# A two-layer hybrid decoder step on one core: low halves of the dense weights written in place, four high halves, more PSUM banks, a rearranged first norm, full-row value products, and a second layer without its meta tokens

## The chip, the cores and the metric

The kernel runs on one core of one Trainium2 chip. The metric is the device time of one execution in microseconds (us). Before the change three runs gave a median of 1439.03 us (1437.47 to 1439.14).

## The reference, cut to what matters

336 token columns go through two layers with the same weights: 16 learned meta tokens, 256 prompt tokens (together one sequence of 272), and 8 samples of 8 new tokens each. Only the prompt tokens and the samples are returned as `y`; of the meta tokens the outputs hold nothing directly.

```python
def mixer_block(x, pos, attend, conv_prev, h_prev, p, l):
    hn = rmsnorm(x, p['ln_mix'][l])
    z = hn @ p['w_in'][l]                       # q, k, v, recurrent x, recurrent gate y, two merge gates
    att, k_state, v_state = attend(l, q, k, v, p['attn_sinks'][l])   # window of 128, sink softmax
    rec, h_last, conv_state = rglru_branch(xr, conv_prev, h_prev, pos, ...)   # conv of 4, two gates, scan
    rec = rec * jax.nn.gelu(yr)
    merged = jax.nn.sigmoid(ga) * (att @ p['w_att_proj'][l]) + jax.nn.sigmoid(gr) * (rec @ p['w_rec_proj'][l])
    return x + merged @ p['w_out'][l], k_state, v_state, conv_state, h_last

for l in range(DEPTH):                          # DEPTH = 2
    x, ... = mixer_block(x, ..., l)
    hf = rmsnorm(x, p['ln_ffn'][l])
    x = x + swiglu(hf, ...) if l % 2 == 0 else x + moe_ffn(hf, ...)   # layer 1: top 2 of 8 experts
return rmsnorm(x, p['ln_final']), ...
...
y_prompt = y_p[:, N_META:]
```

In layer 1 the keys, the values and the recurrent x of the meta tokens are still needed by the prompt tokens behind them (window and scan); their merge gates, their y, their attention output and their merged x are not.

## The kernel before, in words

All activations lie with the features on the 128 partitions and the tokens as columns. Every dense product is made in three passes of rounded 32-bit matmuls (fp32r): a weight w is split into a high part (w rounded to fp32r) and a low part (w less that), an activation likewise, and `three` issues high x high, high x low and low x high into one PSUM bank. The weights stream from HBM in chunks of 512 KB (128 x 1024 values: 8 tiles of 128 x 128). For each chunk c:

- SyncE loads it into one of four `raw` buffers (`RING = 4`). It may load over a slot when the low part of the chunk four before is done (`lo_done`).
- ScalarE's `hi(c)` rounds it into one of two `whi` buffers (`SPLIT = 2`), which must have been released by TensorE: it waits until chunk c-2 is multiplied (`pe_chunk`).
- VectorE's `lo(c)` subtracts and writes one of two `wlo` buffers. In the gate stage `hi_lo(c)` does both on VectorE.
- TensorE's `chunk(c)` makes 24 matmuls, 3 for each tile, and raises `pe_chunk`.

A layer's chunks are numbered: 20 for k, v, recurrent x and q (0 to 19), 16 merge gates, 8 for the block-diagonal gates of the recurrence (`N_G`, 360 columns each), 10 for y (`C_Y`), 8 attention projection (`C_A`), 10 recurrent projection (`C_R`), 8 output projection (`C_O`). After layer 0 come 72 chunks of the dense FFN; after layer 1 the router and the experts, with their own rings (`mraw`, `mwhi`; there the low part `mwlo` is already written over `mraw`).

Each engine's program is written out in a fixed order; engines meet through semaphores alone. What matters for the change:

- First norm. The first 12 chunks multiply x times the gain, unnormalised, and VectorE scales the result by 1/rms afterwards. Layer 0's sum of squares is made on ScalarE (`square`), added on GpSimd (`add_squares`), summed over partitions on TensorE inside chunk 2 (`sums`), and goes through `root` (ScalarE) and `reciprocal` (VectorE). Four banks hold the results until then. VectorE then also computes `softplus` of a small tensor in one piece in step 9.
- Attention, step s: TensorE makes scores of unit s+1, one weight chunk, `turn(s)` (transposes of the weights) and `values(s-1)`. VectorE makes `maxima`, `weights`, `lo` and in some steps `conv(t)`, one tenth of the convolution. 17 units of kinds A, B, C, D. In C and D the values of the new tokens (`vp[0:16, 2]`, `vnew` with 8 rows) are multiplied with 16 or 8 rows of the array, between products with 128 rows.
- Recurrence. While the y and attention-projection chunks run, ScalarE makes three functions per tenth (`factors`), a square root in two pieces and the gelu of `yr` in two halves; VectorE multiplies and scans; GpSimd multiplies hs by yr (`rect`); ScalarE and VectorE split `rect` into `rech` and `recl`, which the recurrent projection reads. VectorE also takes each chunk's result out of PSUM, and does that ahead of `lo(c+2)`. Two banks alternate.

Of the kernel before, what the change touches and what calls it, by code (L numbers as in the profile page):

```python
# [18 lines left out]
F32 = mybir.dt.float32  # L19
# [7 lines left out]
P = 128  # L27
# [43 lines left out]
RING, SPLIT = 4, 2  # L71
# [16 lines left out]
ATT_N = {"A": 4, "B": 2, "C": 2, "D": 2}  # L88
SINK0 = {"A": 0, "B": 16, "C": 32, "D": 34}
# [25 lines left out]
def build_step(nc, w_mix, w_ffn, w_moe, x_in, consts_in, par_in, misc_in, state_in, kc_in, vc_in,  # L115
               o_y, o_kp, o_vp, o_ks, o_vs, o_state):
    with ExitStack() as ctx:
# [29 lines left out]
        vnew = at("vnew", [SS, SB, P], F32, I_)  # L147
# [110 lines left out]
        k_ready, vt_mm, v_ready = sem("k_ready"), sem("vt_mm"), sem("v_ready")  # L258
# [50 lines left out]

        def gain(n):  # L310
            return lnf if n == 4 else p_(n // 2, "ln_ffn" if n % 2 else "ln_mix")

        def att_part(u):
# [7 lines left out]
            first = 2 * P if kind == "C" else TP + 16 * i  # L321
            return qkx[:, 0:KD, first:first + 16], o[:, 0:P].rearrange("p (h s) -> p h s", h=KD)
# [5 lines left out]
        def _(sy):  # L328
            sy.dma_start(raw[:, 0, :], w_mix[0, 0]).then_inc(raw_loaded[0], 16)
# [3 lines left out]
            sy.dma_start(raw[:, 1, :], w_mix[0, 1]).then_inc(raw_loaded[1], 16)  # L333
            sy.dma_start(cst[:, 0:256], consts_in[:, 0:256]).then_inc(consts_loaded, 16)

            def stream(src, c0, n):

                first = 0
                if c0 == 0:
                    for j in range(2, RING):  # L340
                        sy.dma_start(raw[:, j, :], src[j]).then_inc(raw_loaded[j], 16)
# [3 lines left out]
                with sy.Fori(first // 4, n // 4) as i:  # L345
                    for j in range(4):
                        sy.wait_ge(lo_done, i * 4 + (c0 + j + 1 - RING))
                        sy.dma_start(raw[:, (c0 + j) % RING, :], src[i * 4 + j]).then_inc(raw_loaded[(c0 + j) % RING], 16)
# [3 lines left out]
            stream(w_mix[1], BASE[1], N_MIX)  # L352
# [3 lines left out]
            for j in range(MRING):  # L356
                if j == N_EARLY:
# [22 lines left out]
        def _(pool):  # L380
# [11 lines left out]
            for l in range(2):  # L392
# [21 lines left out]

                pool.wait_ge(z_evac, z0 + 1)
# [20 lines left out]
                pool.dma_start(o_vs[l, WIN - SS:WIN], vnew[:, :, :]).then_inc(kv_out_done, 16)  # L436

                pool.wait_ge(o_evac, NU * (l + 1))
                for k in range(KD):
                    pool.wait_ge(att_hi, 2 * l + k // 4 + 1)  # L440
                    pool.tensor_tensor(attl[:, k, :], qkx[:, k, :], atth[:, k, :].bitcast(F32), ALU.subtract).then_inc(att_lo, 1)

                for t in range(KR):
# [3 lines left out]
                    pool.tensor_tensor(rect[:, t, 0:TP], hs[:, t, 0:TP], yr[:, t, 0:TP], ALU.mult)  # L447
# [1502 lines left out]
```

## Time and profile before

| | |
|---|---|
| median of 3 runs | 1439.03 us |
| the profiled execution: its own time | 1435.18 us |
| its span (first to last instruction) | 1433.3 us |
| granted TensorE clock, mean | 0.996 |
| TensorE busy / VectorE / ScalarE / GpSimd | 97% / 75% / 58% / 11% |

A page of the profile groups instructions by line and tile. Two things are needed to read it here. The ends of matmuls are modelled and overlap their successors: a 336-column matmul is shown with 0.32 us, but the next one starts 0.153 us later, so the rate is read from starts, not from durations. And an idle time in front of a matmul is counted from that modelled end, so the matmul starts later than an unbroken stream would have it by the idle time and about 0.16 us more.

### The profile page before, as it was taken

Reading aid. Unit: us, or ns where it says so; the run is one execution under the profiler, and the core shown is the slowest. Engines: PE = TensorE matmul, PEld = TensorE weight load, DVE = VectorE, ACT = ScalarE, POOL = GpSimd, SP = SyncE. Lnnn points to the kernel's source line nnn. Section 1 sums busy time; section 2 is a strip of 40 time slices with the busy share of each in tenths; the row PEclk is TensorE's granted clock in tenths of the full one; section 3 lists DMA queues with packets and bytes.
Section 4 is the critical chain, followed back from the end, with each engine's and each line's share of the span. In section 5 each row is a group of like instructions: output and inputs, shape, how many; then the busy total and the mean of one; then the engine's idle time right before and its main releaser. Section 6 shows DMA issues by size and latency. Waiting matters only on the chain.

```text
span 1433.3 us, 24028 instructions
## 1 busy us (share of the span) xinstructions
PE 1388.4 (97%) x8258; PEld 1267.7 (88%) x8258; DVE 1081.6 (75%) x1593; ACT 827.9 (58%) x1221; POOL 155.1 (11%) x175
## 2 busy tenths in 40 slices
PE   6999999899999999999999999999999999999997
PEld 5988899899999999999888998996888888888885
DVE  5678776977666664556687769765998998998987
ACT  4356547734433333343565477345888888888884
POOL 2010002311100000100000023112120120011010
PEclk9999999999999999999999999999999999999999
DMA  6443244354545454444332344468999999999991
GB/s 231 132 136 103 89 118 147 118 151 136 178 138 144 145 146 138 141 146 140 131 104 89 118 147 118 145 234 296 401 396 385 408 367 368 409 374 369 401 334 54
DMA packets 83256, 298.28 MB, mean 208 GB/s; under 512 B 9568, under 2 KB 10848, under 8 KB 83168
## 3 DMA queue, kind: packets, MB, share of 16 engines
q1 hardware_dynamic: 77760, 278.39, 56.1%
q0 software_dynamic: 5408, 18.72, 4.3%
q8 instruction: 55, 0.90, 0.3%
q14 instruction: 33, 0.27, 0.1%
HBM read 285.50 MB, written 11.58 MB: 207 GB/s over the span
## 4 chain that ended last, share of the span: by engine, by line
PE 79%; DVE 13%; issue 4%; ACT 3%; POOL 0%; DMA 0%; ACTq 0%; DVEq 0%; SPq 0%; POOLq 0%
PE ps L1385 17%; PE ps L1387 17%; PE ps L1386 17%; PE ps L1676 7%; PE ps L1680 7%; PE ps L1677 7%; DVE mwlo L940 3%; DVE wlo L875 3%; ACT whi L531 1%; PE ps L1484 1%; DVE hs L1088 1%; ACT mwhi L531 1%; PE ps L1500 1%; PE ps L1460 1%; DVE htl L1345 1%
## 5 line engine op out<-in xcount | busy, mean ns | idle before, releaser
L875 DVE TENSOR_TENSOR wlo<-raw,whi 128x1024 fp32r<-128x1024 f32 x232 | 288.5, 1243 | 185.1 <-ACT whi L531 184.3
L531 ACT ACTIVATE whi<-raw 128x1024 fp32r<-128x1024 f32 x216 | 228.5, 1058 | 335.9 <-PE ps L1387 332.9
L940 DVE TENSOR_TENSOR mwlo<-mraw,mwhi 128x1024 fp32r<-128x1024 f32 x290 | 345.0, 1222 | 35.2 <-ACT mwhi L531 30.4
L531 ACT ACTIVATE mwhi<-mraw 128x1024 fp32r<-128x1024 f32 x290 | 304.1, 1060 | 61.5 <-PE ps L1680 59.1
L1385 PE MATMUL ps<-xuh,whi 128*128 128x336 f32 x576 | 184.6, 320 | 12.5 <-DVE xul L887 8.0
L1386 PE MATMUL ps<-xul,whi 128*128 128x336 f32 x576 | 182.7, 317 | 0.0
L1387 PE MATMUL ps<-xuh,wlo 128*128 128x336 f32 x576 | 182.5, 317 | 0.0
L1385 PE MATMUL ps<-xnh,whi 128*128 128x336 f32 x544 | 176.7, 325 | 4.8 <-DVE wlo L875 4.0
L1387 PE MATMUL ps<-xnh,wlo 128*128 128x336 f32 x544 | 172.4, 317 | 0.0
L1386 PE MATMUL ps<-xnl,whi 128*128 128x336 f32 x544 | 172.0, 316 | 0.0
L1676 PE MATMUL ps<-mwhi,xeh 128*128 128x512 f32 x384 | 152.7, 398 | 0.9 <-ACT xeh L531 0.9
L1680 PE MATMUL ps<-mwhi,xel 128*128 128x512 f32 x384 | 149.9, 390 | 0.0
L1677 PE MATMUL ps<-mwlo,xeh 128*128 128x512 f32 x384 | 149.6, 390 | 0.0
L1385 PEld LDWEIGHTS ps<-xuh,whi 128*128 128x128 f32 x576 | 109.4, 190 | 13.3 <-issue 8.0
L1385 PEld LDWEIGHTS ps<-xnh,whi 128*128 128x128 f32 x544 | 102.3, 188 | 14.5 <-issue 12.0
L1386 PEld LDWEIGHTS ps<-xul,whi 128*128 128x128 f32 x576 | 109.7, 190 | 0.3
L1387 PEld LDWEIGHTS ps<-xuh,wlo 128*128 128x128 f32 x576 | 109.4, 190 | 0.0
L1386 PEld LDWEIGHTS ps<-xnl,whi 128*128 128x128 f32 x544 | 102.6, 189 | 0.0
L1387 PEld LDWEIGHTS ps<-xnh,wlo 128*128 128x128 f32 x544 | 102.1, 188 | 0.0
L1680 PEld LDWEIGHTS ps<-mwhi,xel 128*128 128x128 f32 x384 | 72.1, 188 | 15.8 <-DVE xel L1308 0.4
L1676 PEld LDWEIGHTS ps<-mwhi,xeh 128*128 128x128 f32 x384 | 72.2, 188 | 15.0 <-issue 1.1
L1677 PEld LDWEIGHTS ps<-mwlo,xeh 128*128 128x128 f32 x384 | 72.2, 188 | 14.0
(310 smaller groups left out, 2667.7 us busy)
## 6 DMA issues: line engine op xcount, KB each, us to landing
mraw<-w_moe SPq DMA_DIRECT2D x292, 512.0 KB, 8.0
raw<-w_mix SPq DMA_DIRECT2D x160, 512.0 KB, 3.6
raw<-w_ffn SPq DMA_DIRECT2D x72, 512.0 KB, 3.6
x<-x_in SPq DMA_DIRECT2D x4, 336.0 KB, 5.6
tok_d<-xt POOLq DMA_DIRECT2D x6, 224.0 KB, 4.8
ysum_d<-zero POOLq DMA_DIRECT2D x3, 448.0 KB, 10.9
ysum<-ysum_d POOLq DMA_DIRECT2D x3, 448.0 KB, 10.2
o_y<-nt SPq DMA_DIRECT2D x8, 168.0 KB, 1.9
```

Source lines behind the costliest of these rows:

```text
L531: return nc.scalar.activation(out, in_, ACT.Copy)
L875: v.tensor_tensor(wlo[c % SPLIT][:, :, :], raw[:, c % RING, :].rearrange("p (k n) -> p k n", n=P), f32(whi[c % SPLIT][:, :, :]), ALU.subtr ...
L940: v.tensor_tensor(mwlo[q % MRING][:, :, :], mraw[q % MRING][:, :].rearrange("p (k n) -> p k n", n=512), f32(mwhi[q % MSPLIT][:, :, :]), AL ...
L1088: v.tensor_tensor_scan(hs[:, t, :], rg[:, t, :], ig[:, t, :], 0.0, ALU.mult, ALU.add).then_inc(scan_done, 1)
L1345: v.tensor_tensor(htl[n % 2][:, :, :], ps[4][:, :].rearrange("p (k n) -> p k n", k=4), f32(hth[n % 2][:, :, :]), ALU.subtract).then_inc(ht ...
L1385: mm(out, wh, xh, start=start, stop=False)
L1386: mm(out, wh, xl, start=False, stop=False)
L1387: return mm(out, wl, xh, start=False, stop=stop)
L1460: ins = mm(bank[:, 0:256], qkx[r, k, 128:256], qkx[r, 8, 0:256], start=True, stop=True)
L1676: mm(out, lhs_h, hi[:, n, :], start=start, stop=False)
L1677: mm(out, lhs_h, lo[:, n, :], start=False, stop=False)
L1680: return mm(out, lhs_l, hi[:, n, :], start=False, stop=stop)
```

## The change

- `lo` writes `wlo` over its own `raw` slot; the freed room makes four `whi`. `hi` waits for TensorE no more (its slot is free when the new chunk has been loaded); the load itself now waits for `pe_chunk` of the chunk four before instead of `lo_done`. The last four chunks of layer 1 are loaded between the first expert loads.
- The first 12 chunks use 6 banks instead of 4; layer 0's sum of squares goes from chunk 2 to chunk 3; chunks 4 and 5 are split ahead of the root; `softplus` is spread over three steps. y and attention projection use 4 banks, the recurrent projection two others.
- In y, the projections and the output VectorE does `lo(c+2)` ahead of taking chunk c's result. `conv(1)` leaves step 16 of the projections; `conv(1)` to `conv(8)` stand at steps 3, 6, 9, 11, 13, 15, 17, 18 of the attention.
- `vp[:, 2]` and `vnew` get 128 rows, cleared by GpSimd, and the value products of units C and D use all of them. A D unit's output is laid out by sample, so that it is contiguous.
- In layer 1, from the merge gates on, the 16 meta columns are left out (`kept(l)`): 320 columns instead of 336.

```diff
-RING, SPLIT = 4, 2
+RING = 4
+N_BANKS = 6
+CONV_AT = (3, 6, 9, 11, 13, 15, 17, 18)
...
-        raw = at("raw", [P, RING, CH], F32, 10752)
-        whi = [at(f"whi{i}", [P, 8, P], F32R, 27136 + 8192 * i) for i in range(SPLIT)]
-        wlo = [at(f"wlo{i}", [P, 8, P], F32R, 31232 + 8192 * i) for i in range(SPLIT)]
+        raw = [at(f"raw{i}", [P, CH], F32, 10752 + 4096 * i) for i in range(RING)]
+        wlo = [at(f"wlo{i}", [P, 8, P], F32R, 10752 + 4096 * i) for i in range(RING)]
+        whi = [at(f"whi{i}", [P, 8, P], F32R, 27136 + 4096 * i) for i in range(RING)]
...
+        def kept(l):
+            return slice(META if l else 0, T)
... SyncE
-                        sy.wait_ge(lo_done, i * 4 + (c0 + j + 1 - RING))
+                        sy.wait_ge(pe_chunk, i * 4 + (c0 + j + 1 - RING))
...
+                if j in (4, 6, 8, 10):
+                    c = N_MIX - RING + j // 2 - 2
+                    sy.wait_ge(pe_chunk, BASE[1] + c + 1 - RING)
+                    sy.dma_start(raw[(BASE[1] + c) % RING][:, :], w_mix[1, c])...
... GpSimd
+                pool.wait_ge(pe_chunk, BASE[l] + N_U)
+                if l == 0:
+                    pool.memset(vp[:, 2, :], 0.0).then_inc(v_zero, 1)
+                pool.memset(vnew[:, :, :], 0.0).then_inc(v_zero, 1)
... ScalarE, hi
-                if c >= SPLIT:
-                    act.wait_ge(pe_chunk, i * step + (c - SPLIT + 1))
-                copy(whi[c % SPLIT][:, :, :], raw[:, c % RING, :]...
+                copy(whi[c % RING][:, :, :], raw[c % RING][:, :]...
... ScalarE, start of layer 0
             hi(3)
+            act.wait_ge(eps_set, 1)
+            nc.scalar.activation(rms3[:, 0:1], eps[:, :], ACT.Sqrt)
+            hi(4)
+            hi(5)
... VectorE, first norm
-                    if l == 0 and j == 0:
-                        lo(c0 + 3)
+                    else:
+                        for c in {0: (2, 3, 4, 5), 1: (6,), 3: (7,)}.get(j, (j + 3,) if 5 <= j <= 10 else ()):
+                            lo(c)
... VectorE, y (attention projection alike)
+                    lo(c0 + C_Y + t + 2)
                     ve.wait_ge(pe_chunk, c0 + C_Y + t + 1)
-                    v.tensor_copy(yr[:, t, :], ps[t % 2][:, 0:T]).then_inc(z_evac, 1)
-                    lo(c0 + C_Y + t + 2)
+                    v.tensor_copy(yr[:, t, kept(l)], ps[t % 4][:, kept(l)]).then_inc(z_evac, 1)
... TensorE, values
                         elif kind == "C":
-                            few = TP - 256
                             mm(ps[7][r, 0:128], vp[:, 1, r], pt[q][:, g, :], start=True, stop=False)
-                            ins = mm(ps[7][r, 0:128], vp[0:few, 2, r], pt[q][0:few, 2 + g, :], start=False, stop=True)
+                            ins = mm(ps[7][r, 0:128], vp[:, 2, r], pt[q][:, 2 + g, :], start=False, stop=True)
                         else:
                             for i in range(2):
-                                out = ps[7][r, 0:128].rearrange("p (h i s) -> p h i s", i=2, s=SS)[:, :, i, :]
+                                out = ps[7][r, 64 * i:64 * i + 64]
                                 mm(out, vc[:, b, r], pt[q][:, i, r], start=True, stop=False)
-                                ins = mm(out, vnew[:, b, r], pt[q][0:SS, 2 + i, r], start=False, stop=True)
+                                ins = mm(out, vnew[:, b, r], pt[q][:, 2 + i, r], start=False, stop=True)
... TensorE, merge gates of layer 1 (y and the projections alike)
-                        chunk(c0 + C_I + s, ps[s % 2][:, 0:T], xnh, xnl)
+                        tokens = kept(l) if s >= 2 else slice(0, T)
+                        chunk(c0 + C_I + s, ps[s % 2][:, tokens], xnh[:, :, tokens], xnl[:, :, tokens])
```

Where the order of an engine's instructions moves, at the two places on which most rests. First VectorE at the start of layer 0, in the kernel before (`wlo` is the low part of a chunk, `rstd` the reciprocal, `qkx<-ps,rstd` the scaled result of a chunk, `nt` and `xnl` the norm of one feature tile):

```order
L875 TENSOR_TENSOR wlo_53<-raw,whi_51 128x1024
L875 TENSOR_TENSOR wlo_54<-raw,whi_52 128x1024
L892 RECIPROCAL rstd<-rms 128x336
L967 TENSOR_TENSOR qkx<-ps,rstd 128x336
L895 SCALAR_TENSOR_TENSOR nt<-x,par,rstd 128x336
L967 TENSOR_TENSOR qkx<-ps,rstd 128x336
L895 SCALAR_TENSOR_TENSOR nt<-x,par,rstd 128x336
L900 TENSOR_TENSOR xnl<-nt,xnh 128x336
L875 TENSOR_TENSOR wlo_53<-raw,whi_51 128x1024
```

And the same place now:

```order
L898 TENSOR_TENSOR wlo_56<-raw_52,whi_60 128x1024
L898 TENSOR_TENSOR wlo_57<-raw_53,whi_61 128x1024
L898 TENSOR_TENSOR wlo_54<-raw_50,whi_58 128x1024
L898 TENSOR_TENSOR wlo_55<-raw_51,whi_59 128x1024
L914 RECIPROCAL rstd<-rms 128x336
L995 TENSOR_TENSOR qkx<-ps,rstd 128x336
L917 SCALAR_TENSOR_TENSOR nt<-x,par,rstd 128x336
L898 TENSOR_TENSOR wlo_56<-raw_52,whi_60 128x1024
```

The low parts of chunks 4 and 5 moved from behind the reciprocal and the first evacuations to ahead of it.

Second, VectorE in the attention projection of a layer (`gates<-ps,gates` takes a chunk's result out, `hs` is the scan, `recl` the low part of the recurrent output), before:

```order
L1116 TENSOR_TENSOR gates<-ps,gates 128x336
L875 TENSOR_TENSOR wlo_54<-raw,whi_52 128x1024
L1108 TENSOR_TENSOR recl<-rect,rech 128x336 x3
L1088 SCALAR_TENSOR_TENSOR hs<-rg,ig 128x360 x2
L1116 TENSOR_TENSOR gates<-ps,gates 128x336
L875 TENSOR_TENSOR wlo_53<-raw,whi_51 128x1024
L1108 TENSOR_TENSOR recl<-rect,rech 128x336 x2
```

And now:

```order
L898 TENSOR_TENSOR wlo_57<-raw_53,whi_61 128x1024
L1143 TENSOR_TENSOR gates<-ps,gates 128x336
L1134 TENSOR_TENSOR recl<-rect,rech 128x336 x3
L1114 SCALAR_TENSOR_TENSOR hs<-rg,ig 128x360 x2
L898 TENSOR_TENSOR wlo_54<-raw_50,whi_58 128x1024
L1143 TENSOR_TENSOR gates<-ps,gates 128x336
L1134 TENSOR_TENSOR recl<-rect,rech 128x336 x2
```

The low part of chunk c+2 stands ahead of the wait for chunk c, where it stood behind.

## Rows read from the trace of the kernel before

**Rows 1.** The page: each engine's busy us, share of the span, instructions.
```profile
PE 1388.4 (97%) x8258; PEld 1267.7 (88%) x8258; DVE 1081.6 (75%) x1593; ACT 827.9 (58%) x1221; POOL 155.1 (11%) x175
```

**Rows 2.** Windows: length, busy us (count) of PE, PEld, DVE, ACT, POOL, PEclk, DMA, GB/s.
```profile
400.00:600.00 200.00, 200.00 (x1307) 200.00 (x1306) 117.46 (x164) 71.75 (x85) 4.43 (x4) 1.00 0.48 144
256.00:295.00 39.00, 34.71 (x217) 32.95 (x217) 38.06 (x46) 26.24 (x36) 19.43 (x23) 1.00 0.43 128
866.00:905.00 39.00, 34.72 (x217) 32.95 (x216) 38.01 (x46) 26.23 (x36) 19.42 (x23) 1.00 0.44 129
```

**Rows 3.** Timeline of TensorE, first norm: start, us, line, tiles, shape [idle before <-releaser].
```profile
23.01 0.83 PE L1392 MATMUL ps<-acc,cst 128*128 128x336 f32 x2 [2.38 <-POOL acc L390]
...
31.83 0.42 PE L1385 MATMUL ps<-xuh,whi 128*128 128x336 f32 x1 [3.86 <-DVE wlo L875]
...
32.90 0.48 PE L1387 MATMUL ps<-xuh,wlo 128*128 128x336 f32 x1
33.18 0.48 PE L1385 MATMUL ps<-xuh,whi 128*128 128x336 f32 x1
...
63.83 0.41 PE L1385 MATMUL ps<-xnh,whi 128*128 128x336 f32 x1 [0.83 <-DVE qkx L967]
```

**Rows 4.** Windows at the attention's start, both layers; then VectorE's timeline there.
```profile
80.00:106.00 26.00, 24.36 (x175) 22.43 (x175) 19.83 (x51) 14.45 (x48) 0.51 (x1) 1.00 0.34 103
134.00:155.00 21.00, 21.00 (x153) 18.63 (x150) 18.37 (x50) 12.47 (x36) 0.00 (x0) 1.00 0.33 101
690.00:716.00 26.00, 22.98 (x163) 21.17 (x163) 18.44 (x49) 14.31 (x45) 0.52 (x1) 1.00 0.27 89
...
89.03 0.46 DVE L987 TENSOR_SCALAR xc<-ext,par 128x360 f32<-128x360 f32 x1
...
92.25 1.22 DVE L875 TENSOR_TENSOR wlo<-raw,whi 128x1024 fp32r<-128x1024 f32 x1
```

**Rows 5.** Timeline of TensorE: value products of units B, C, D, and what follows.
```profile
155.72 0.67 PE L1500 MATMUL ps<-pt,vp 128*64 128x128 f32 x8
156.32 0.33 PE L1458 MATMUL ps<-kc,qt 64*64 64x136 f32 x2
...
166.83 0.43 PE L1503 MATMUL ps<-pt,vp 128*64 128x128 f32 x2
...
168.27 0.33 PE L1458 MATMUL ps<-kc,qt 64*64 64x136 f32 x2
...
173.23 0.33 PE L1509 MATMUL ps<-pt,vc 128*64 128x64 f32 x2
...
175.28 0.45 PE L1458 MATMUL ps<-kc,qt 64*64 64x136 f32 x4
```

**Rows 6.** Timeline of TensorE: idle in gate stage, y stage, and start of the FFN.
```profile
208.54 0.43 PE L1385 MATMUL ps<-xch,whi 128*128 128x360 f32 x1 [0.76 <-DVE wlo L875]
...
229.36 0.39 PE L1385 MATMUL ps<-xnh,whi 128*128 128x336 f32 x1 [0.30 <-DVE wlo L875]
...
373.83 0.42 PE L1385 MATMUL ps<-xuh,whi 128*128 128x336 f32 x1 [0.58 <-DVE wlo L875]
```

**Rows 7.** Timelines of ScalarE and GpSimd: the recurrence's chain in layer 0.
```profile
271.71 1.61 ACT L714 ACTIVATE yr<-yr 128x1680 f32<-128x1680 f32 x1
...
273.40 0.79 POOL L447 TENSOR_TENSOR rect<-hs,yr 128x272 f32<-128x272 f32 x1 [29.41 <-ACT yr L714]
...
291.20 0.60 POOL L448 TENSOR_TENSOR rect<-hs,yr 128x64 f32<-128x64 f32 x1
```

**Rows 8.** Timeline of TensorE in the gate stage, first and last of 20 matmuls.
```profile
202.82 0.32 PE L1386 MATMUL ps<-xcl,whi 128*128 128x360 f32 x1
...
205.96 0.33 PE L1387 MATMUL ps<-xch,wlo 128*128 128x360 f32 x1
```

**Rows 9.** The page: weight loads, count, KB each, median us from issue to landing.
```profile
mraw<-w_moe SPq DMA_DIRECT2D x292, 512.0 KB, 8.0
raw<-w_mix SPq DMA_DIRECT2D x160, 512.0 KB, 3.6
```

More of the change, by code:

```diff
@@ L900, in normal_low, with softplus @@
                 v.tensor_tensor(xnl[:, k, :], nt[:, k, :], f32(xnh[:, k, :]), ALU.subtract).then_inc(xlo_done, 1)
-            def softplus():
+            def softplus(part):
                 a, b = PAR["lam"]
@@ L907, in softplus @@
                 two = lambda t: t[:, :].rearrange("p (l k) -> p l k", l=2)
-                v.scalar_tensor_tensor(out=two(sp_e), in0=lam, scalar=-1.0, in1=lam, op0=ALU.mult, op1=ALU.max).then_inc(c_ready, 1)
-                step(v.tensor_scalar(two(sp_q), lam, -1.0, 0.0, ALU.mult, ALU.max))
-                a, b = PAR["sinks"]
-                step(v.tensor_scalar(nsink[:, :].rearrange("p (l k) -> p l k", l=2), par[:, :, a:b], -1.0, None, ALU.mult))
-                ve.wait_ge(sp_exp, 1)
-                step(v.tensor_scalar(sp_p[:, :], sp_e[:, :], 2.0, None, ALU.add))
@@ L914, in softplus @@
-                step(v.reciprocal(sp_z[:, :], sp_p[:, :]))
-                step(v.tensor_tensor(sp_z[:, :], sp_z[:, :], sp_e[:, :], ALU.mult))
-                step(v.tensor_tensor(sp_e[:, :], sp_z[:, :], sp_z[:, :], ALU.mult))
-                step(v.tensor_scalar(sp_p[:, :], sp_e[:, :], 1.0 / 15, None, ALU.mult))
-                for d in (13, 11, 9, 7, 5, 3):
-                    step(v.scalar_tensor_tensor(out=sp_p[:, :], in0=sp_p[:, :], scalar=1.0 / d, in1=sp_e[:, :], op0=ALU.add, op1=ALU.mult))
@@ L971, in _ @@
                         normal_low(l, j - 1)
-                    if l == 0 and j == KD + 1:
-                        softplus()
+                    if l == 0 and j > KD:
+                        softplus(j - KD - 1)
                 def lines():
@@ L1051, in _ @@
                         lo(c0 + C_I + s + 1)
-                    if s % 3 == 0 and 3 <= s <= 15:
-                        conv(1 + s // 3)
-                    if s >= 17:
-                        conv(s - 10)
+                    if s in CONV_AT:
+                        conv(CONV_AT.index(s) + 1)
                     if s == 5:
@@ L1131, in _ @@
                     c = c0 + C_R + j
+                    lo(c + 2)
                     done = m < KD and (KR * m + KR - 1) // 8 == j
@@ L1401, in chunk @@
                         sum_squares(sums)
-                    ins = three(out, whi[c % SPLIT][:, k, :], wlo[c % SPLIT][:, k, :], xh[:, k, :], xl[:, k, :],
+                    ins = three(out, whi[c % RING][:, k, :], wlo[c % RING][:, k, :], xh[:, k, :], xl[:, k, :],
                                 start and k == 0, stop and k == 7)
@@ L1407, in _ @@
                 c0, u0 = BASE[l], NU * l
[L1408 to L1417 removed]
+                for j in range(N_U):
+                    if j >= N_BANKS:
+                        pe.wait_ge(z_evac, N_IN * l + j - N_BANKS + 1)
+                    if l == 0 and j == 3:
+                        pe.wait_ge(consts_loaded, 16)
+                    chunk(c0 + j, ps[j % N_BANKS][:, 0:T], xuh, xul, ready=None if j else xu_lo, count=16 * l,
+                          sums=2 * l if j == (0 if l else 3) else None)
                 pe.wait_ge(xlo_done, KD * (l + 1))
[L1419 to L1422 removed]
+                for j in range(N_U, C_I - 2):
+                    pe.wait_ge(z_evac, N_IN * l + j - 1)
+                    chunk(c0 + j, ps[j % 2][:, 0:T], xnh, xnl)
                 pe.wait_ge(z_evac, N_IN * l + 2)
```

185 lines of the change are left out of this document (95 added, 90 removed).

## The prediction, made before the changed kernel had run

> **What bounds the kernel now.** I read the page first: TensorE is busy 97% of the span [rows 1], no other engine comes near. In the windows, a stretch without a wait (the FFN) shows 1307 matmuls in 200 us, 0.153 us each, at the full clock [rows 2]. So two things shorten this kernel: less work on TensorE, or fewer of its waits. Then I listed TensorE's idle time in the timeline. It sits at few places: the first norm [rows 3], the start of the attention [rows 4], single waits at the gate and y stages and at the FFN [rows 6], and above all the stretch 256 to 295 and its twin in layer 1, where 217 matmuls, 33.5 us of work at 154.5 ns (that stage's rate), take 39 us [rows 2]. Last, the attention's value products: TensorE is called busy there, but the starts show that it advances slowly [rows 5].
>
> The sum is made against the profiled execution (1435.2 us with 1.9 us around its span); the median is 3.8 us above it, and I add the same to the forecast. Each wait is charged as its idle time plus 0.16 us for the modelled tail of the matmul before.
>
> **The change, part by part.**
>
> First norm. Chunk 2 waits 2.38 us for GpSimd's sums, chunk 4 waits 3.86 us for the low part that stands behind the reciprocal, and after that gap TensorE's granted clock is at the lower level: starts 0.28 us apart instead of 0.153, for some twelve matmuls [rows 3]. Now the sum stands at the end of chunk 3 (about 24 us; the sums were ready at 23.0, and ScalarE reaches its squares earlier), and six banks carry TensorE over chunks 4 and 5 to 32.7 us. By then VectorE must have lo(4), lo(5), the reciprocal, one result and lo(6). Chunk 4's load is issued when chunk 0 is multiplied (13.6 us), and lands beside the cache loads, say by 21; hi(5) by 24, root by 26, reciprocal by 28.5, lo(6) by 31. That fits with 1.7 us to spare. Gain: 2.54 + 4.02 + 12 x 0.13 = 8.1 us. The wait at 63.83 (0.83) is for chunk results held up by `softplus` in one piece; with it in three: 1.0 us. Together 9.1; at least 6.0, if the root is 3 us later than I think.
>
> Start of the attention. The idle time is 1.64 us in layer 0 (two waits) and 3.02 in layer 1 (three) [rows 4]. VectorE does conv(1) from 89.03 to 92.25, 3.2 us, just ahead of the low part and the maxima that TensorE wants [rows 4]. Gone from there, no wait is left: 4.66 + 5 x 0.16 = 5.5 us. The convolutions now stand denser from step 9 on. A stretch of 21 us, 3.8 steps with one convolution, has VectorE busy 18.4 us [rows 4]; with one in every second step it is 18.4 + 0.9 x 3.2 = 21.3 us of work in 21 us. That just fits, since the units C and D behind it cost VectorE less. At least 3.
>
> Value products. B units: four products of 128 columns, all with 128 rows, and the next line starts 0.60 us after the first (the two heads' chains side by side, 8 records). C: the same columns, but 128 and 16 rows by turns, 1.44 us. 
>
> The trace shows that loads with equal rows run ahead and those with changing rows don't. The Trainium skill ("TensorE: Matmul & The Clock Gate", Part 3, the mechanism) says nearly the opposite: a weight load overlaps a running matmul only when its row group differs. By that rule full rows win nothing, and the sum is 12.9 us less; the B and C rows speak against it.
>
> Gate and y stages. A wait of 0.76 in each layer, where `hi_lo` waits for TensorE and conv(9) follows, and 0.30 and about 0.2 in y [rows 6]; with four high parts ready ahead they go: 2 x (0.92 + 0.84) = 3.5 us; at least 1.5. The FFN's start waits 0.58 for a low part behind the reciprocal [rows 6]: 0.7 us.
>
> Recurrence and projections. 5.5 us lost per layer, 11.0 in all [rows 2]. VectorE is busy 38.06 of the 39 us, so it matters whether its work can come earlier. Before the stretch it isn't full (in y it waits for hi, which waits for TensorE), and the order "result, then lo(c+2)" leaves the low part only 1.2 us between its hi and TensorE's need. The long chain is: square root and gelu on ScalarE (the gelu's first half from 271.7), GpSimd's ten products (273.4 to 291.8, full), recl [rows 7]. Without ScalarE's waits for TensorE I get the gelu done at 269 instead of 273.3, GpSimd's last product at 288, the last recl at 290; TensorE, unhindered, begins the recurrent projection at 288.1 and needs the last recl 4.1 us later. On the way the low parts of attention chunks 4 to 6 come 1 to 2.5 us ahead of need. In layer 1 TensorE is faster still, so some wait is left. I take 5.0 + 4.0 = 9.0 us. At least 0, at most 11.8 with the short wait for the banks at the projections' border, 0.4 us a layer.
>
> Layer 1 without meta columns. 16 merge gates, 10 y, 8, 10 and 8 projection chunks: 52 chunks of 24 matmuls, 1248. From 360 columns (0.165 us, [rows 8]) to 336 (0.153 to 0.1545, [rows 2]) a column costs 0.43 to 0.5 ns; at the full clock of 2.4 GHz it is 0.417. With 0.417 x 16 = 6.7 ns: 8.3 us; with 0.5, 9.9. I take 8.4. The other engines do 5% less there.
>
> In place low parts: nothing. The same subtraction is already written over its input in the expert stage, hidden behind matmuls as this one is. The last four loads of layer 1 stand behind four expert loads: at 8.0 us from issue to landing [rows 9] and issued one to four chunks after the output stage begins, each is there more than 5 us before its need. Nothing; the experts' own loads are issued a little later but with a ring of 24 to live on.
>
> Sum: 9.1 + 5.5 + 12.9 + 3.5 + 0.7 + 9.0 + 8.4 = 49.1 us. 1435.2 - 49 = 1386 profiled, 1390 for the median.
>
> **The rivals.**
>
> Rival 1: VectorE bounds the recurrence. For it speaks 38.06 of 39 us; against it the idle it has before. Then the 11 us of waits stay, and the 18 shorter chunks of y and attention projection in layer 1 bring nothing (18 x 0.16 = 2.9): 1390 + 9 + 3 = 1402.
>
> Rival 2: value products don't speed up, because the row change isn't the cause but the 64-column form or the accumulation: D's share gone, C's small: 1390 + 11 to 13 = 1402. For it: D differs from B in more than rows. Against: C differs from B in the rows alone. Rivals 1 and 2 together: 1414.
>
> Rival 3, slower: the ring of raw slots. A slot is now held until TensorE is through with the chunk, and the load is issued only then. Load, hi and lo (landing + 1.06 + 1.23) and the multiplication (3.67) must fit into four chunk times, 14.7 us: from a landing of 8.7 us on every chunk is late. At a landing of 12 us a chunk takes (12 + 2.3 + 3.7) / 4 = 4.5 us instead of 3.67, and 228 chunks lose about 187 us: 1577. It outweighs the 49 us from a landing of 9.6 us on. For it: expert loads land in 8.0 us under a crowd. Against: the dense loads land in 3.6 [rows 9] at half the DMA share.
>
> Rival 4: the change holds, but the new order brings waits of its own at the first norm (root late) and with the denser convolutions: 3 + 2.5 lost, 1396.
>
> **How the numbers follow.** The forecast 50%, with its own range 1385 to 1396 (value products 9.5 to 12.9, recurrence 6 to 11.8, columns 8.3 to 9.9). Rival 4 15%, rival 1 18%, rival 2 12%, rival 3 2%, rivals 1 and 2 together 3%. The range 1384 to 1404 leaves out rival 3, rivals 1 and 2 together, and parts of the others' tails. A difference under 0.2% (2.9 us) can't be told from none here. Faster takes everything but rival 3 and a small rest: 96%; same 2%; slower 2%.
>
> **What would show it.** In the profile after: no idle over 0.3 us on TensorE between 8 and 55 us, and the granted clock full from 12 us on; layer 0's recurrence some 17 us earlier than before. The value lines of C and D as groups of records 0.6 us long. Matmuls of 128x320 in layer 1, 0.146 to 0.148 us apart. The window that answers to 256:295 with 217 matmuls in about 34 us, VectorE nearly as full. The expert stage as long as before. I am wrong if TensorE's idle time in the recurrence stays near 4 us a layer (rival 1), if D's products still show starts 0.26 us apart (rival 2), or if waits for raw loads appear anywhere in the dense part (rival 3).

## The result, and the profile after

The changed kernel takes 1392.39 us (median of 4 runs, 1391.69 to 1394.02) where the kernel before took 1439.09 (4 runs on the same chip). The ratio is 0.968, 95% interval 0.9663 to 0.9696. The forecast was 1390, range 1384 to 1404.

The profiled execution took 1391.69 us (span 1389.9), against 1435.18 before: 43.5 us less, where the sum of the terms said 49.1. The medians differ by 46.7 us. That the two differ goes with the granted clock, below.

The page after, first the busy time of the engines, as in [rows 1], and the weight loads of [rows 9]:

```profile
PE 1361.3 (98%) x8258; PEld 1250.4 (90%) x8258; DVE 1074.4 (77%) x1593; ACT 824.5 (59%) x1222; POOL 158.0 (11%) x178
...
mraw<-w_moe SPq DMA_DIRECT2D x292, 512.0 KB, 8.1
raw<-w_mix SPq DMA_DIRECT2D x160, 512.0 KB, 3.6
```

TensorE runs as many matmuls in 27 us less of busy time; the rest of the gain is idle time. The dense loads land as fast as before, so that the ring of raw slots is no bound (rival 3).

Windows of the changed kernel (length, busy us and count of PE, PEld, DVE, ACT, POOL, then granted clock, DMA share, GB/s): the FFN, the first norm, and the stretches that answer to 256:295 and 866:905 of [rows 2]:

```profile
400.00:600.00 200.00, 200.00 (x1306) 200.00 (x1305) 112.62 (x153) 70.00 (x85) 5.52 (x6) 1.00 0.47 142
8.00:55.00 47.00, 47.00 (x292) 46.81 (x293) 34.11 (x56) 25.76 (x40) 12.96 (x13) 1.00 0.61 201
237.00:271.00 34.00, 31.29 (x200) 30.28 (x199) 33.02 (x40) 23.96 (x32) 17.08 (x18) 1.00 0.42 125
835.00:866.00 31.00, 27.63 (x182) 26.37 (x181) 30.09 (x39) 19.73 (x25) 20.30 (x23) 1.00 0.40 120
```

The FFN is as before (1306 matmuls in 200 us, 1307 before). The first norm has no idle time left, and no fall of the clock: the starts are 0.28 us apart until 12.6 us, where they were in the kernel before until 12.0, and 0.153 from there on. But the recurrence stretch still has 2.71 us without a matmul in layer 0 and 3.37 in layer 1, with VectorE busy 97% of it. There the forecast fell short. TensorE's waits after, by what ended them (line, releaser, us in total, times, longest):

```profile
PE ps L1407 <- DVE xul L909: 8.0, 1, 8.0
PE ps L1407 <- DVE wlo L898: 5.8, 5, 2.4
```

The 8.0 us are the start of the kernel. The five waits for low parts are all in the two recurrences. TensorE's timeline (start, us, line, tiles, shape, idle before) names them:

```profile
256.50 0.40 PE L1407 MATMUL ps<-atth,whi 128*128 128x336 f32 x1 [0.32 <-DVE wlo L898]
266.72 0.40 PE L1407 MATMUL ps<-atth,whi 128*128 128x336 f32 x1 [2.39 <-DVE wlo L898]
...
843.39 0.41 PE L1407 MATMUL ps<-atth,whi 128*128 128x320 f32 x1 [0.30 <-DVE wlo L898]
847.62 0.38 PE L1407 MATMUL ps<-atth,whi 128*128 128x320 f32 x1 [0.44 <-DVE wlo L898]
857.62 0.39 PE L1407 MATMUL ps<-atth,whi 128*128 128x320 f32 x1 [2.40 <-DVE wlo L898]
```

To place the gain I set the start of each chunk's last matmul side by side in both traces. The difference grows, stage by stage, as the third column says. The fourth and fifth tell what each part costs when it alone is undone (the experiments below), by the medians and by the chunks' ends; in the fifth the falls of the granted clock in the recurrences, 1.5 us each, are left out.

| stage | forecast | by the traces | undone alone, medians | undone alone, traces |
|---|---|---|---|---|
| first norm | 9.1 | 9.2 | 9.1 | 7.4 |
| attention start | 5.5 | 5.2 | 5.6 | 3.2 |
| value products C, D | 12.9 | 1.7 + 9.2 = 10.9 | 11.5 | 10.9 |
| gate and y stages, FFN start, borders of stages | 4.2 | 4.5 | with the next row: 8.8 | with the next row: 9.4 |
| recurrence and attention projection | 9.0 | 4.4 | | |
| 16 columns in layer 1 | 8.4 | 9.1 | 8.9 | 8.0 |
| sum | 49.1 | 43.3 | 43.9 | 38.9 |

### The profile page after: what moved, and what is told of

Its sections match the earlier page's. It is cut to its first block, busy times and chain, and to the rows that moved or that the text cites. A ratio compares the mean times of both kernels' runs of the same rounds, so it can differ in the third digit from the quotient of the medians.

```text
span 1389.9 us, 23721 instructions
## 1 busy us (share of the span) xinstructions
PE 1361.3 (98%) x8258; PEld 1250.4 (90%) x8258; DVE 1074.4 (77%) x1593; ACT 824.5 (59%) x1222; POOL 158.0 (11%) x178
## 4 chain that ended last, share of the span: by engine, by line
PE 85%; DVE 9%; issue 3%; ACT 2%; DMA 0%; ACTq 0%; DVEq 0%; SPq 0%
PE ps L1407 19%; PE ps L1409 19%; PE ps L1408 19%; PE ps L1694 8%; PE ps L1698 7%; PE ps L1695 7%; DVE mwlo L967 3%; DVE wlo L898 1%; PE ps L1502 1%; DVE hs L1114 1%; ACT mwhi L549 1%; PE ps L1478 1%; PE ps L1518 1%; DVE htl L1367 1%; DVE ig L1101 1%
## 5 line engine op out<-in xcount | busy, mean ns | idle before, releaser
L1407 PE MATMUL ps<-xnh,whi 128*128 128x336 f32 (+1 forms) x544 | 174.5, 321 | 0.0
L1409 PE MATMUL ps<-xnh,wlo 128*128 128x336 f32 (+1 forms) x544 | 170.7, 314 | 0.0
L1408 PE MATMUL ps<-xnl,whi 128*128 128x336 f32 (+1 forms) x544 | 170.6, 314 | 0.0
```

The lines of the kernel that those rows point to most:

```text
L1407: mm(out, wh, xh, start=start, stop=False)
L1408: mm(out, wh, xl, start=False, stop=False)
L1409: return mm(out, wl, xh, start=False, stop=stop)
```

## The experiments

Each kernel is the changed one with one edit. Differences are against its median of 1392.4. The kernel before, run beside each set, had medians of 1436.4 to 1436.9 (9 runs each) where it had 1439.1 beside the changed kernel, so a difference between sets is good to 2 or 3 us; a kernel with an edit worth nothing, the second one here, came out at 1392.1.

**Few rows again.**

```diff
-    ins = mm(ps[7][r, 0:128], vp[:, 2, r], pt[q][:, 2 + g, :], start=False, stop=True)
+    ins = mm(ps[7][r, 0:128], vp[0:few, 2, r], pt[q][0:few, 2 + g, :], start=False, stop=True)
...
-        ins = mm(out, vnew[:, b, r], pt[q][:, 2 + i, r], start=False, stop=True)
+        ins = mm(out, vnew[0:SS, b, r], pt[q][0:SS, 2 + i, r], start=False, stop=True)
```

> The changed kernel with the value products of units C and D on 16 and 8 rows again (the layout of D's output stays contiguous). Theory (the alternation of row counts makes each product start late): C units 0.86 us longer twice, D units 1.15 us longer eight times, as the two traces show: 10.9 us slower than the changed kernel, 1403, with D's starts 0.26 us apart. Rival (the form of D's output, or its accumulation, is the cause): D's share stays gained, only C's 1.7 us come back, 1394. Second rival (nothing of it counts, another wait takes it up): 1392.

Measured: 1403.84 us (1403.57 to 1407.47), 11.5 slower; ratio to the kernel before 0.9774 (0.976 to 0.9787). TensorE's timeline of one D unit in this kernel, to the scores behind it:

```profile
162.86 0.33 PE L1527 MATMUL ps<-pt,vc 128*64 128x64 f32 x2
163.12 0.32 PE L1528 MATMUL ps<-pt,vnew 8*64 8x64 f32 x2
163.37 0.33 PE L1527 MATMUL ps<-pt,vc 128*64 128x64 f32 x2
...
164.65 0.32 PE L1528 MATMUL ps<-pt,vnew 8*64 8x64 f32 x2
164.91 0.68 PE L1476 MATMUL ps<-kc,qt 64*64 64x136 f32 x8
```

Each product with another row count starts 0.26 us after the one ahead; the unit takes 2.05 us, as before. The same unit in the changed kernel:

```profile
161.34 0.33 PE L1526 MATMUL ps<-pt,vc 128*64 128x64 f32 x2
161.51 0.28 PE L1527 MATMUL ps<-pt,vnew 128*64 128x64 f32 x2
161.63 0.33 PE L1526 MATMUL ps<-pt,vc 128*64 128x64 f32 x4
...
162.24 0.68 PE L1476 MATMUL ps<-kc,qt 64*64 64x136 f32 x8
```

0.90 us. Rival 2 of the prediction is out.

**Strided output.** Full rows, but D's output laid out by head again.

```diff
-    out = ps[7][r, 64 * i:64 * i + 64]
+    out = ps[7][r, 0:128].rearrange("p (h i s) -> p h i s", i=2, s=SS)[:, :, i, :]
```

> The changed kernel with D's output laid out by head again, so that each product writes eight pieces of eight columns 16 apart, but all rows full. Theory (rows decide alone): no change, within 1 us of the changed kernel, 1392. Rival (the strided output decides): 8 x 1.15 = 9.2 us slower, 1401.6.

Measured: 1392.12 us (1391.43 to 1392.79); ratio 0.9687 (0.9674 to 0.97). The D unit takes 0.90 us with the strided output too. The contiguous layout brings nothing; the rows do it.

**All columns in layer 1.** `kept(l)` returns `slice(0, T)`.

> The changed kernel with all 336 columns in layer 1. Theory (time is columns, for TensorE sets the pace everywhere): 52 chunks x 0.15 to 0.20 us by the traces, 9.3 us slower, 1401.7, and every stage by its own share. Rival (part of it is lost in the waits of the recurrence, where VectorE is full, so that shorter chunks there bring nothing): the 18 chunks of y and attention projection of layer 1 contribute 2.9 us less, 1399, and the waits of layer 1's recurrence are shorter than with 320 columns by as much.

Measured: 1401.33 us (1400.78 to 1402.16), 8.9 slower; ratio 0.9753 (0.9739 to 0.9766). The stages show both theories at work. The 16 merge gates of layer 1 cost 0.19 us each and the y chunks 0.20, but over the eight chunks of attention projection the distance to the changed kernel grows by only 0.1 us, once 1.5 us for a fall of the clock is taken off. There shorter chunks only wait longer: about 1.2 us of the 9.3 expected are lost, the y chunks' share is not.

**The first norm undone**: four banks, the sum of squares in chunk 2, low parts of chunks 4 and 5 behind the reciprocal, softplus in one piece.

```diff
-N_BANKS = 6
+N_BANKS = 4
...
-            hi(4)
-            hi(5)
...
-                          sums=2 * l if j == (0 if l else 3) else None)
+                          sums=2 * l if j == (0 if l else 2) else None)
```

> The changed kernel with the first norm as it was: four banks, the sum of squares in chunk 2, the low parts of chunks 4 and 5 behind the reciprocal, softplus in one piece. Theory: the three waits and the drop of the granted clock come back, 9.2 us slower, 1401.6, with the granted clock near half between 31 and 36 us. Rival (the four high parts alone, which free ScalarE and VectorE from waiting for TensorE, remove most of it): 3 us slower or less, 1395.

Measured: 1401.45 us (1399.57 to 1401.9), 9.1 slower; ratio 0.9754 (0.9741 to 0.9768). Its windows at the first norm, PE alone (busy, count, granted clock, DMA share, GB/s):

```profile
30.00:32.00 2.00, 2.00 (x11) 0.80 0.00 0
32.00:34.00 2.00, 2.00 (x9) 0.50 0.00 0
34.00:36.00 2.00, 2.00 (x13) 0.85 0.00 0
```

The lower level is back. By the chunks' ends 7.4 us return by chunk 4 and nothing behind it. The wait for GpSimd's sums is 1.33 us where it was 2.38, and the wait at 63.83 in [rows 3] does not come back, though `softplus` stands in one piece again: another part of the change removes that one too, most likely the four high parts, which no run here shows alone. The profiled execution loses another 1.5 us to a fall of the clock in layer 0's recurrence, which the changed kernel's didn't have. So that the medians give 9.1, as the forecast said, is partly luck.

**The convolutions where they stood.**

```diff
-                    if s in CONV_AT:
-                        conv(CONV_AT.index(s) + 1)
+                    if s % 3 == 0 and 3 <= s <= 15:
+                        conv(1 + s // 3)
+                    if s >= 17:
+                        conv(s - 10)
```

> The changed kernel with the convolutions where they stood: conv(1) in the projections, the others from step 3 on by threes and in the last steps. Theory: the waits at the attention's start come back (1.9 us in layer 0, 3.1 in layer 1), 5 us slower, 1397.4, and TensorE idle near the start of the attention again. Rival (the four high parts give VectorE's low parts enough room anyway): 1 us, 1393.5.

Measured: 1398.02 us (1396.16 to 1398.44), 5.6 slower; ratio 0.9725 (0.9712 to 0.9738). By the chunks' ends 0.9 us come back in layer 0 and 2.3 in layer 1 at the attention's start, 3.2 of the 5 expected: a part of this gain stays without moving the convolutions. The profiled execution has a fall of the clock in each recurrence besides, 1.5 us apiece, which is more than the rest of the 5.6.

**The order undone in y and attention projection.**

```diff
-                    lo(c + 2)
                     ve.wait_ge(pe_chunk, c + 1)
...
                     v.tensor_tensor(gates[:, j, kept(l)], ps[j % 4][:, kept(l)], gates[:, j, kept(l)], ALU.mult)...
+                    lo(c + 2)
```

> The changed kernel with the order 'result, then low part of chunk c+2' again on VectorE in y and attention projection. Theory (the low part has only 1.2 us of slack behind the result, and VectorE is full from 251 to 277): the first waits of the recurrence grow by a low part's 1.2 us in several chunks, and the change loses 2 to 4 us, 1395.5. Rival (VectorE has the same work in either order, so the order moves waits but makes none): within 1 us, 1392.

Measured: 1397.44 us; ratio 0.9724 (0.971 to 0.9737). The five runs are 1392.98 (the profiled one, mean clock 0.998) and 1396.5 to 1397.7 (0.994 and 0.995). In the profiled one the chunks' ends slip 1.2 us in each layer's recurrence, 2.3 in all, which is within the theory; that the others are 4 us longer goes with their lower mean clock, but they have no trace.

**Two high parts again, the rest as changed.**

```diff
+                if c >= 2:
+                    act.wait_ge(pe_chunk, i * step + (c - 1))
                 copy(whi[c % RING][:, :, :], raw[c % RING]...
```

> The changed kernel with the high part waiting again until TensorE is through with chunk c-2, as it must with two buffers; all else as changed. Theory (this wait is what tied ScalarE and VectorE to TensorE and made the waits of gate stage, y and recurrence): the waits of the gate stage (0.9 a layer) and y (0.5 a layer) come back, and ScalarE's chain to the gelu is 3 to 5 us later, so that the recurrence waits 4 us more in all; 7 us slower, 1399, the first norm's gain partly lost beside it. Rival (the order and the banks made the gain, not the high parts): within 1.5 us, 1393.

Measured: 1420.44 us (1418.87 to 1421.11), 28 slower, not 7; ratio 0.9883 (0.9868 to 0.9898). Neither theory. TensorE's waits in this kernel, the four that say why:

```profile
PE ps L1410 <- DVE wlo L900: 9.7, 11, 2.4
...
PE ps L1410 <- DVE gates L1165: 4.8, 6, 1.1
...
PE ps L1410 <- issue: 3.0, 1, 3.0
PE ps L1410 <- DVE mgl L1170: 2.1, 2, 1.1
```

TensorE now waits for results and their splits (`gates`, `mgl`), which it doesn't in the changed kernel. The timeline without TensorE's own rows, inside the recurrent projection:

```profile
287.33 1.06 ACT L549 ACTIVATE whi<-raw 128x1024 fp32r<-128x1024 f32 x1 [2.23 <-PE ps L1412]
...
288.50 1.23 DVE L900 TENSOR_TENSOR wlo<-raw,whi 128x1024 fp32r<-128x1024 f32 x1 [1.68 <-ACT whi L549]
```

The high part waits for TensorE, the low part for the high part, and the result behind them can't begin before 289.7, 2.4 us after the high part was let go. Another 5.9 of the 28 us lie at the first norm: a wait of 3.0 us at 57.88 (the row `issue`), and behind it matmuls at the lower clock (granted 0.50 from 58 to 62 us). Then I put the order back too:

**Two high parts and the old order** (two high parts from chunk 14 on, so that the first norm stays as changed; the old order in y, in all three projections and in the FFN).

```diff
+                if c >= 14:
+                    act.wait_ge(pe_chunk, i * step + (c - 1))
...
-                    lo(c + 2)
                     ve.wait_ge(pe_chunk, c + 1)
                     v.tensor_tensor(...)
+                    lo(c + 2)
```

> The changed kernel with the high part waiting for TensorE's chunk c-2 from chunk 14 on (the first norm is left as changed), and with the low parts standing where they stood in the kernel before in y, the three projections and the FFN. The run with the wait alone lost 28 us. Theory (high parts and order belong together: with two high parts a low part ahead of the result holds the result back by a high and a low part, 2.3 us, with the old order it doesn't): most of the 28 us goes away, what stays is what four high parts and order together gained, 9 us by the stages' ends in the two traces, 11.6 us by what the four undone parts leave of the 46.7; 1401 to 1404. Rival (the wait for chunk c-2 by itself costs it, whatever the order, and the kernel before had hidden it in waits that are gone now): 1412 or more.

Measured: 1401.2 us (1400.87 to 1401.57), 8.8 slower; ratio 0.9753 (0.9739 to 0.9766). The theory holds. By the chunks' ends of the two kernels, recurrent and output projection, in layer 0 with the FFN's first chunk, lose 0.5 us in layer 0 with the old order and 6.8 with the new one, in layer 1 0.3 and 5.2. That is 11.2 of the 19.2 us between the two kernels; 1.8 more lie in the FFN, and 5.9 in the first norm, which this kernel leaves alone, so that part isn't tested.

The 8.8 us and the four undone parts above make 43.9 us by the medians, and by the kernel before as it ran beside these sets the whole change is worth 44.0 to 44.5. That they agree is partly luck. The profiled executions of the four kernels with rows, columns, first norm or convolutions undone have seven falls of the clock in their recurrences, 1.5 us each; the changed kernel's has none. Without them the parts make 38.9 us, where the whole made 43.3. So some 4 us are held by more than one part, and undoing one alone doesn't bring them back: 1.8 at the first norm, 2.0 at the attention's start, about 1.1 of the columns.

**GpSimd beside VectorE.** 36 additions of 128x128 on GpSimd in each layer, from 222.5 to 253.6 us in layer 0, where it otherwise idles.

```diff
+                for n in range(36):
+                    pool.wait_ge(busy_pool, 37 * l + n + 1)
+                    pool.tensor_tensor(zero[:, :], zero[:, :], zero[:, :], ALU.add).then_inc(busy_pool, 1)
```

> One look. 36 additions of 128x128 on GpSimd are put ahead of its products of the recurrence in each layer, where it otherwise idles; nothing else changes. Theory (a tensor operation of GpSimd slows VectorE's beside it: low parts took 1.52 us beside them and 1.22 without): VectorE's low parts beside the additions take 1.4 to 1.6 us, its other operations a fifth longer, and the recurrence's waits grow by 1 to 4 us. Rival (the low parts in that stretch are longer for a reason of their own, such as ScalarE reading or the DMA writing the same memory): 1.22 us as before, time within 1 us of 1391.7.

Measured: 1396.05 us, one run, 4.4 over the changed kernel's profiled execution. VectorE in this kernel, beside the additions:

```profile
235.71 2.44 DVE L1106 TENSOR_TENSOR ig<-ig,mul 128x2160 f32<-128x2160 f32 x1
...
238.51 1.45 DVE L903 TENSOR_TENSOR wlo<-raw,whi 128x1024 fp32r<-128x1024 f32 x1
239.89 0.49 DVE L1128 COPY yr<-ps 128x336 f32<-128x336 f32 x1
240.30 2.81 DVE L1119 TENSOR_TENSOR_SCAN hs<-rg,ig 128x360 f32<-128x360 f32 x3
```

And the same instructions in the changed kernel, with GpSimd idle:

```profile
236.25 2.41 DVE L1101 TENSOR_TENSOR ig<-ig,mul 128x2160 f32<-128x2160 f32 x1
...
238.96 1.23 DVE L898 TENSOR_TENSOR wlo<-raw,whi 128x1024 fp32r<-128x1024 f32 x1
240.10 0.50 DVE L1123 COPY yr<-ps 128x336 f32<-128x336 f32 x1
240.52 2.49 DVE L1114 TENSOR_TENSOR_SCAN hs<-rg,ig 128x360 f32<-128x360 f32 x3
```

This low part takes 0.22 us more, a scan 0.11, the long product and the read from PSUM nothing. Of seven low parts beside the additions five took 1.31 to 1.45 us and two stayed at 1.23. By the chunks' ends layer 0's recurrence is 2.8 us later, 1.5 of them a fall of the clock, and layer 1's 2.0 without one. So VectorE is slowed beside GpSimd, unevenly, and it costs time in this stretch.

The Trainium skill ("SBUF — State Buffer", Who interferes with whom) says that an instruction of VectorE with two inputs in SBUF contends with a GpSimd instruction that reads SBUF, and one with at most one doesn't. The low parts, the scans and the reads from PSUM agree; the product of two SBUF tiles (2.44 for 2.41 us) and the two low parts at 1.23 don't.

**Two squares ahead.** What is the stretch's bound? ScalarE's timeline in the changed kernel:

```profile
231.48 2.01 ACT L721 ACTIVATE mul<-mul 128x2160 f32<-128x2160 f32 x1 [2.69 <-DVE mul L1110]
248.56 1.41 ACT L734 ACTIVATE mul<-mul 128x1440 f32<-128x1440 f32 x1 [2.72 <-DVE mul L1110]
252.23 1.61 ACT L739 ACTIVATE yr<-yr 128x1680 f32<-128x1680 f32 x1
```

and VectorE's:

```profile
230.12 0.51 DVE L1123 COPY yr<-ps 128x336 f32<-128x336 f32 x1 [1.38 <-PE ps L1409]
230.55 0.90 DVE L1110 SCALAR_TENSOR_TENSOR mul<-asq,mul 128x720 f32<-128x720 f32 x1
234.47 1.22 DVE L898 TENSOR_TENSOR wlo<-raw,whi 128x1024 fp32r<-128x1024 f32 x1 [3.02 <-ACT whi L549]
```

The square root waits for VectorE's product at 230.55, which stands behind a result that waits for TensorE; then VectorE waits 3 us for the high part behind that root. The edit takes the product ahead:

```diff
+                    if t == 6:
+                        squares(2)
                     lo(c0 + C_Y + t + 2)
                     ve.wait_ge(pe_chunk, c0 + C_Y + t + 1)
...
+                    if j == 0:
+                        squares(4)
                     lo(c + 2)
                     ve.wait_ge(pe_chunk, c + 1)
```

> The changed kernel with two of VectorE's squares (the factors' squares ahead of ScalarE's square roots) placed ahead of the low part and the result that they stood behind. The changed kernel's trace has ScalarE idle 2.7 us before each of two square roots, and VectorE idle 3.0 us at 231.5 for the high part behind the first. Theory (the chain square, root, gelu, GpSimd's ten products, low part of the recurrence ends in the 2.4 us wait at 266.7, and these idle times are on it): the chain comes 2 to 3 us earlier in each layer and the wait shrinks by as much; 3 to 5 us faster than the changed kernel, 1388, and the granted clock stays full there. Rival (VectorE's throughput bounds the stretch, slowed by GpSimd's products beside it): the wait stays at 2.4 us, 1392.

Measured: 1387.94 us (1385.95 to 1388.14), 4.4 faster; ratio to the kernel before 0.9658 (0.9644 to 0.9671). ScalarE in this kernel:

```profile
229.16 2.01 ACT L721 ACTIVATE mul<-mul 128x2160 f32<-128x2160 f32 x1
...
245.55 1.41 ACT L734 ACTIVATE mul<-mul 128x1440 f32<-128x1440 f32 x1
249.22 1.61 ACT L739 ACTIVATE yr<-yr 128x1680 f32<-128x1680 f32 x1
```

The gelu starts 3.0 us earlier, 3.3 when the 0.3 us that this execution started later are taken off, and TensorE's waits in layer 0 shrink to one:

```profile
264.38 0.39 PE L1409 MATMUL ps<-atth,whi 128*128 128x336 f32 x1 [0.78 <-DVE wlo L898]
```

By the chunks' ends it gains 2.7 us in layer 0, and in layer 1 1.3 with a fall of the clock there (2.9 in the kernel with both edits below, where the clock stayed). So most of what was missing is the chain's latency, not VectorE's throughput.

**Heads by turns in D.**

```diff
+                    if kind == "D":
+                        for i in range(2):
+                            for g in range(2):
+                                mm(out, vc[:, b, r], pt[q][:, i, r], start=True, stop=False)
+                                ins = mm(out, vnew[:, b, r], pt[q][:, 2 + i, r], start=False, stop=True)
```

> The changed kernel with the products of a D unit issued head by turn (sample outside, head inside), the same 16 products. In the changed kernel's trace the second head's chain starts 0.29 us after the first; in B units the two heads alternate and start 13 ns apart. Theory (half the array works alone for the first and last 0.29 us): 0.25 us less for each D unit, eight of them, 2 us faster, 1390.4, the unit in 0.65 us instead of 0.90. Rival (TensorE issues one product every 0.055 us or slower whichever half it uses, and 16 of them take 0.9 us in any order): 1392.4.

Measured: 1391.64 us (1390.78 to 1392.15), 0.8 faster; ratio 0.9686 (0.9672 to 0.9699). The unit in this kernel:

```profile
161.67 0.34 PE L1517 MATMUL ps<-pt,vc 128*64 128x64 f32 x4
161.83 0.29 PE L1518 MATMUL ps<-pt,vnew 128*64 128x64 f32 x4
161.95 0.33 PE L1517 MATMUL ps<-pt,vc 128*64 128x64 f32 x4
162.07 0.33 PE L1518 MATMUL ps<-pt,vnew 128*64 128x64 f32 x4
162.33 0.68 PE L1476 MATMUL ps<-kc,qt 64*64 64x136 f32 x8
```

0.66 us instead of 0.90, and by the chunks' ends 0.93 us in each layer, 1.9 in all. The medians show less than sets can differ by; one reason is in the windows behind the 2.4 us wait of layer 0, those of this kernel (here the profiled execution is the median one):

```profile
263.00:269.00 6.00, 3.63 (x15) 3.39 (x14) 6.00 (x7) 3.04 (x5) 6.00 (x6) 0.74 0.30 88
```

and of the changed kernel:

```profile
263.00:269.00 6.00, 3.61 (x24) 3.36 (x23) 6.00 (x8) 3.13 (x5) 6.00 (x7) 1.00 0.40 120
```

The clock fell in this execution and not in the other, which took back 1.5 us.

**Both together.** The squares and the heads.

> Both edits together. Theory: they add, 5 to 7 us faster than the changed kernel, 1386. Rival (either is hidden): the better of the two alone.

Measured: 1385.53 us (1384.41 to 1385.76), 6.9 faster than the changed kernel; ratio to the kernel before 0.9643 (0.963 to 0.9656). They add: 2.4 us more than the squares alone. It is the fastest version I ran. TensorE's waits for low parts in it:

```profile
PE ps L1409 <- DVE wlo L898: 2.6, 2, 1.8
```

## Why the prediction was right, and where its sum was off

The forecast and its direction held, and no rival's number came; but the sum was 5.8 us too high by the traces, and the addition for the median hid a part of that. By its own steps:

- First norm: 9.2 for 9.1. Chunks 4 and 5 never wait, and the clock doesn't fall; undone, it costs 9.1 by the medians but 7.4 by the chunks' ends.
- Attention start: 5.2 for 5.5. All waits are gone, and the denser convolutions bring none (rival 4). But not all of it is the convolutions': with them alone undone 3.2 us of waits come back.
- Value products: 10.9 for 12.9. C behaves like B, 0.86 us each for 0.84. D gains 1.15 and not 1.4: its two heads' chains overlap only by half, 0.90 us where B's units take 0.60. My lower bound of 1.0 was for chains one behind the other, so this is between. With the heads by turns the unit takes 0.66.
- The Trainium skill ("TensorE: Matmul & The Clock Gate", Part 3, The mechanism) has a sentence by which a weight load overlaps a running matmul only when its row group differs. Here products with equal rows overlap (0.90 us for a D unit), and those with alternating rows take 0.26 us each (2.05 us), in the kernel with few rows again as in [rows 5]; the measurement decides against that sentence, for loads of these shapes.
- Gate and y stages with the FFN's start: 4.0 for 4.2, and 0.5 more at the borders of the projections, which I had put into the upper bound of the recurrence only.
- **Recurrence: 4.4 for 9.0. This is the term that was mis-sized.** I let ScalarE's chain run ahead by freeing it of TensorE, and had the gelu 4.3 us earlier against TensorE. It starts at 252.23 where it started at 271.71 [rows 7], 19.5 us earlier, but TensorE itself is 18.1 us ahead in the y stage: 1.4 us gained, not 4.3. What I missed is that ScalarE doesn't only wait for TensorE itself: its two square roots wait for a product that VectorE does behind a result from TensorE. With that product moved, 2.7 and 2.9 us came by the chunks' ends, 5.6 in all and more than the 4.6 that were missing. The sign that I had named, 217 matmuls in about 34 us, didn't come: the window 237:271 above has 200. Rival 1's sign was idle time near 4 us a layer, and 2.7 and 3.4 us are closer to it than to none. But its reason, VectorE's throughput, isn't what held the stretch: the same work on VectorE in another order took the time away. VectorE is slower beside GpSimd, which I hadn't counted: 1.3 to 2 us a layer when it was provoked for 31 us. It isn't new with the change, though: low parts beside GpSimd's products of the recurrence take 1.56 us on average in the changed kernel (ten) and 1.54 in the kernel before (eight). How much time it costs unprovoked, no run tells.
- Columns: 9.1 for 8.4 by the traces, 0.15 to 0.20 us a chunk; undone, 8.9 by the medians and 8.0 by the chunks' ends. What rival 1 says of shorter chunks holds for the attention projection of layer 1 alone, 1.2 us.
- In place low parts and the four high parts beside them: the forecast said nothing of what they are worth together with the order. The runs tell: the pair, with the waits that it removes in gate stage, y and recurrence, is worth 8.8 us; with two high parts the new order is 13 us worse than the old one by the chunks' ends behind the first norm (the other 5.9 of the 19.2 us lie in the first norm, where the two kernels differ in their high parts), and with four high parts the old order in y and attention projection costs 2.3 us by the trace.
- Median: I added 3.8 us for the distance between profiled execution and median. After the change it is 0.7. The longest executions have the lower mean clocks: the changed kernel 1391.69 at 0.998 and 1394.02 at 0.996, the kernel before from 1434.84 at 0.996 to 1439.03 at 0.992. So the 3.8 look like a draw of the clock (the median runs have no trace), and adding them offset a part of the error of the sum (1386 forecast, 1391.7 measured, for the profiled execution). That the median came within 2.4 us of the forecast is luck to that extent.

## What to carry to other kernels

When a wait on the bounding engine is taken away, follow the freed engine's program instruction by instruction, and ask of each wait whom it waits for in turn: ScalarE was freed of TensorE in one place, and still bound to it through VectorE in another. A deeper buffer and an order that uses it are one change: behind the first norm, reordered consumers with the shallow buffer lost 22 us, where undoing both lost 9. Parts undone one by one needn't add up to the whole: here 4 us of 43 were held by more than one part, and falls of the clock in the medians hid it. And in an execution without a profile of its own, a difference of 1 to 4 us may be the clock: compare traces stage by stage before a median is explained.

## What the runs showed of the hardware that I had not expected

- A wait of TensorE of 2.4 us was followed by a fall of the granted clock in some executions and not in others. Nine of the kernels (all but those with the squares moved and the old orders) have this wait in both layers' recurrences. Behind 10 of these 18 waits two or three 2-us windows have less than the full clock, the lowest of them 0.50 to 0.57, so down to the lower level (1.2 GHz), and the chunks behind come 1.5 us later. Behind the other eight, the two of the changed kernel among them, the clock stays at 2.4 GHz. With the squares moved layer 1 still has a wait of 1.79 us; the clock fell behind it in one of the two kernels. So a wait of this size costs up to 1.5 us more than its idle time.
- With row counts that alternate between 128 and 8 each product starts 0.26 us after the one ahead; strided output of eight columns costs nothing (0.90 us for the unit in either form).
- Products of the two heads (64 columns of the array each) run side by side throughout only when they are issued by turns: 0.66 us for a D unit's sixteen records, 0.90 when each half's eight come in one piece.
- VectorE's low part took 1.23 us with GpSimd idle, up to 1.45 beside its additions, and up to 1.80 beside its products of the recurrence.
